# Three of four weight sums from GpSimd to VectorE, and a new order of the VectorE and ScalarE programs in a Strassen-like up projection

## The reference

```python
f_gate, f_val = jnp.split(x @ w_up, 2, axis=-1)          # x: 544 x 1024, w_up: 1024 x 5632
ffn_ext = jnp.concatenate([ffn_hist, f_gate], axis=1)    # two rows of history before the frames
f = gelu(causal_dwconv(ffn_ext, ffn_conv_w, ffn_conv_b)) * f_val      # width 3, 2816 channels
x = layer_norm(DN_ALPHA * x + f @ w_down, ln2_g, ln2_b)
```

## Time and profile before

| | us |
|---|---|
| median of 3 runs | 1791.38 (1789.69 to 1792.2) |
| the profiled execution | 1789.32 |
| its span, first to last instruction | 1787.6 |
| PE busy in the span | 1744.7 (98%) |
| DVE busy | 1372.1 (77%) |
| ACT busy | 856.1 (48%) |
| POOL busy | 350.0 (20%) |

### The profile page before, as it was taken

How to read it: one execution, slowest core, us unless ns; L and a number is a source line. 1 busy time by engine, 2 the same in 40 slices (tenths; PEclk the granted TensorE clock), 3 DMA queues, 4 the chain that set the end, 5 groups by cost and what they waited for, 6 DMA issues and landing times.

```text
span 1787.6 us, 32649 instructions
## 1 busy us (share of the span) xinstructions
PE 1744.7 (98%) x13802; PEld 1702.0 (95%) x13802; DVE 1372.1 (77%) x1869; ACT 856.1 (48%) x1366; POOL 350.0 (20%) x311
## 2 busy tenths in 40 slices
PE   9999999999999999999999999999999999999997
PEld 9998999999998999999999989999999999999997
DVE  5698677755779999876768887786558789998665
ACT  4256533353555555554542564323534655556443
POOL 0025100000135555200000350000001545551000
PEclk9999999999999999999999999999999999999999
DMA  5522122223222222345525221222232222223544
GB/s 173 170 97 72 41 91 74 87 89 97 97 74 88 94 85 83 105 165 179 170 96 170 73 95 36 85 95 71 93 121 72 71 90 79 93 94 111 183 165 137
DMA packets 36514, 186.00 MB, mean 104 GB/s; under 512 B 7376, under 2 KB 11728, under 8 KB 18192
## 3 DMA queue, kind: packets, MB, share of 16 engines
q1 hardware_dynamic: 34672, 176.28, 29.5%
q10 hardware_dynamic: 1696, 7.64, 1.2%
HBM read 176.75 MB, written 7.15 MB: 103 GB/s over the span
## 4 chain that ended last, share of the span: by engine, by line
PE 47%; DVE 10%; issue 4%; POOL 3%; DMA 2%; ACT 2%; ACTq 0%; DVEq 0%; POOLq 0%
PE acc L1995 13%; PE acc L2001 13%; PE acc L2000 13%; DVE cbuf L1763 2%; DMA raw<-wup 2%; DVE slo L1830 2%; DVE fst L1766 2%; POOL sraw L575 1%; PE score L1995 1%; PE score L2001 1%; POOL sraw L578 1%; PE score L2000 1%; DVE wl L1825 1%; DVE cbuf L1769 1%; POOL raw L577 1%
## 5 line engine op out<-in xcount | busy, mean ns | idle before, releaser
L1995 PE MATMUL acc<-xh,wh 128*128 128x272 f32 x1928 | 565.1, 293 | 1.6 <-DVE xl L1163 1.0
L2001 PE MATMUL acc<-xh,wl 128*128 128x272 f32 x1928 | 555.6, 288 | 0.0
L2000 PE MATMUL acc<-xl,wh 128*128 128x272 f32 x1928 | 554.8, 288 | 0.0
L1995 PEld LDWEIGHTS acc<-xh,wh 128*128 128x128 f32 x1928 | 363.1, 188 | 9.7 <-issue 5.0
L1209 DVE TENSOR_TENSOR wl<-raw,wh 128x2048 fp32r<-128x2048 f32 (+2 forms) x118 | 236.1, 2001 | 171.6 <-ACT wh L607 171.0
L2000 PEld LDWEIGHTS acc<-xl,wh 128*128 128x128 f32 x1928 | 363.2, 188 | 0.1
L2001 PEld LDWEIGHTS acc<-xh,wl 128*128 128x128 f32 x1928 | 362.2, 188 | 0.0
L607 ACT ACTIVATE wh<-raw 128x2048 fp32r<-128x2048 f32 (+2 forms) x138 | 236.5, 1714 | 160.8 <-DMA raw<-wdn 113.7
L1995 PE MATMUL acc<-fhh,wh 128*128 128x272 f32 x704 | 204.4, 290 | 2.0 <-DVE wl L1209 2.0
L2000 PE MATMUL acc<-fll,wh 128*128 128x272 f32 x704 | 202.4, 288 | 0.0
L2001 PE MATMUL acc<-fhh,wl 128*128 128x272 f32 x704 | 202.4, 287 | 0.0
(11 more groups left out here) (322 smaller groups left out, 4214.5 us busy)
## 6 DMA issues: line engine op xcount, KB each, us to landing
raw<-win SPq DMA_DIRECT2D x50, 1024.0 KB, 5.0
raw<-wup SPq DMA_DIRECT2D x44, 1024.0 KB, 4.9
raw<-wdn SPq DMA_DIRECT2D x32, 1024.0 KB, 4.8
raw<-wbr SPq DMA_DIRECT2D x24, 512.0 KB, 3.6
raw<-wdn SPq DMA_DIRECT2D x16, 768.0 KB, 4.2
raw<-wout SPq DMA_DIRECT2D x8, 1024.0 KB, 5.0
v_out<-vfm ACTq DMA_DIRECT2D x2, 1088.0 KB, 9.5
k_out<-k ACTq DMA_DIRECT2D x2, 1088.0 KB, 4.9
```

The source lines that it names most:

```text
L1995: first = mm(out, a, xs[0], start=start, stop=False, skip_group_check=onto)
L2000: mm(out, a, xs[1], start=False, stop=False, skip_group_check=onto)
L2001: return mm(out, b, xs[0], start=False, stop=stop, skip_group_check=onto)
```

## The change

GpSimd makes only the first sum s1 of each quad. VectorE makes the other three (third_sum, second_sum, fourth_sum). It has a new wait in first_sum for the chunk, for product 5 of quad q-2 and for GpSimd's sum (s_one). The sums of quad q+2 are issued in quad q, those of 0 and 1 ahead of the loop. ScalarE copies the last gate rows of two tiles at once (last_rows), in place of four VectorE copies; conv_close waits for it (fst_made). The history copy is one instruction for two tiles. ScalarE converts the first half of a chunk before the second, and both engines' lists have a new order.

```diff
-ACT_ORDER, DVE_ORDER = [], []
-for _q in range(QUADS + 1):
-    ACT_ORDER += [("u3", _q - 1)] if _q else []
-    ACT_ORDER += [("m1", _q)] if _q < QUADS else []
-    ACT_ORDER += [("c12", _q - 1)] if _q else []
-    ACT_ORDER += [("u1", _q)] if _q < QUADS else []
-    DVE_ORDER += [("c22", _q - 1)] if _q else []
-    DVE_ORDER += [("c11", _q)] if _q < QUADS else []
+ACT_ORDER, DVE_ORDER = [("m1", 0)], [("c11", 0)]
+for _q in range(QUADS):
+    ACT_ORDER += [("u1", _q), ("u3", _q)]
+    ACT_ORDER += [("m1", _q + 1)] if _q + 1 < QUADS else []
+    ACT_ORDER += [("c12", _q)]
     DVE_ORDER += [("c21", _q - 1)] if _q else []
     DVE_ORDER += [("f", _q - 1)] if _q and _q % 2 == 0 else []
+    DVE_ORDER += [("c22", _q)]
+    DVE_ORDER += [("c11", _q + 1)] if _q + 1 < QUADS else []
+DVE_ORDER += [("c21", QUADS - 1), ("f", QUADS - 1)]
...
                     if q > 1:
                         pool.wait_ge(prod_full, full_at(r, q - 2, 5))
-                    g.tensor_tensor(s1, a21, a22, ALU.add).then_inc(s_made, 1)
-                    pool.wait_ge(s_made, made + 1)
-                    g.tensor_tensor(a21, a11, a21, ALU.subtract).then_inc(s_made, 1)
-                    g.tensor_tensor(s2, s1, a11, ALU.subtract).then_inc(s_made, 1)
-                    pool.wait_ge(s_made, made + 3)
-                    if q > 1:
-                        pool.wait_ge(prod_full, full_at(r, q - 2, 6))
-                    g.tensor_tensor(s4, a12, s2, ALU.subtract).then_inc(s_made, 1)
...
+                    g.tensor_tensor(sraw[q % 2][:, 0, :].rearrange("p (t n) -> p t n", t=4),
+                                    w[:, 0:4, 1, :], w[:, 4:8, 1, :], ALU.add).then_inc(s_one, 1)
...
+                def last_rows(i):
+                    A(fst[:, 2 * i:2 * i + 2, :].rearrange("p m (g r) -> p m g r", r=2),
+                      gex[:, :, GEX - 2 * (DEC + 2):GEX].rearrange("p m (g r) -> p m g r", g=2)[:, :, :, DEC:DEC + 2],
+                      ACT.Copy).then_inc(fst_made, 1)
...
+                first_blocks(0)
                 second_blocks(0)
-                first_blocks(0)
                 two_sums(0)
                 last_sum(0)
+                conv_gelu(0)
                 turned_x_hi(T1, T4N)
-                conv_gelu(0)
                 conv_gelu(1)
...
+                snapshot("m1", 0, 1, "c11")
+                first_blocks(1)
+                second_blocks(1)
+                for q in range(QUADS):
+                    snapshot("u1", q, 3, "c21")
+                    if q % 2:
+                        first_tap(q - 1)
+                    elif q:
                         conv_gelu(1)
                     two_sums(q + 1)
+                    if q == QUADS - 1:
+                        f_his(0, 0)
+                    snapshot("u3", q, 5, "c22")
+                    if q % 2:
+                        conv_gelu(0)
                     last_sum(q + 1)
-                    if q == QUADS - 1:
+                    if q + 1 < QUADS:
+                        snapshot("m1", q + 1, 1, "c11")
+                    else:
                         hi()
...
+                    first_blocks(q + 2)
+                    top_right(q)
+                    second_blocks(q + 2)
+                    if q + 2 == QUADS:
+                        hi()
+                f_his(0, 1)
+                conv_gelu(1)
                 f_his(0, 2)
...
-                        v.tensor_copy(row(fst, t, 0, 2), gex[:, m, SEQ:SEQ + 2]).then_inc(vec, c.up(vec))
-                        v.tensor_copy(row(fst, t, 2, 4), gex[:, m, GEX - 2:GEX]).then_inc(vec, c.up(vec))
+                        if m == 0:
+                            dve.wait_ge(fst_made, c.take(fst_made))
...
+                def third_sum(q):
+                    if q < QUADS:
+                        a11, a12, a21, a22 = blocks_of(q)
+                        v.tensor_tensor(a21, a11, a21, ALU.subtract).then_inc(s_made, 1)
+
+                def second_sum(q):
+                    if q < QUADS:
+                        a11, a12, a21, a22 = blocks_of(q)
+                        v.tensor_tensor(sum_of(q, 1), sum_of(q, 0), a11, ALU.subtract).then_inc(s_made, 1)
...
+                        v.tensor_tensor(sum_of(q, 2), a12, sum_of(q, 1), ALU.subtract).then_inc(s_made, 1)
...
                 turned_x_lo(T2, T3)
+                first_sum(0)
+                third_sum(0)
+                second_sum(0)
+                fourth_sum(0)
+                first_low(0)
+                back_low(0)
                 skip(range(4))
-                conv_close(1, range(2), False)
-                first_low(0)
-                other_lows(0)
+                conv_close(1, (0,), False)
+                two_lows(0)
+                last_low(0)
+                conv_close(1, (1,), False)
                 turned_x_lo(T1, T4N)
+                first_sum(1)
+                third_sum(1)
+                second_sum(1)
+                fourth_sum(1)
+                left(0, 0)
+                first_low(1)
                 f_products(1)
                 history(2)
...
+                for q in range(QUADS):
                     if q:
                         left(q - 1, 1)
...
+                        first_low(q + 1)
+                    back_low(q + 1)
                     if q % 2:
                         conv_close(2 + q // 2, (0,), False)
+                    elif q:
+                        gated_values(q - 1)
+                    bottom_right(q)
+                    if q == QUADS - 1:
+                        f_lows(0, 0)
+                    first_sum(q + 2)
+                    two_lows(q + 1)
+                    third_sum(q + 2)
+                    second_sum(q + 2)
+                    last_low(q + 1)
+                    fourth_sum(q + 2)
+                    if q + 2 == QUADS:
+                        lo()
+                    if q % 2:
+                        conv_close(2 + q // 2, (1,), False)
+                    if q + 1 < QUADS:
+                        left(q + 1, 0)
+                    if q and q % 2 == 0:
+                        history(2 + q // 2)
+                lo()
+                f_lows(0, 1)
+                left(QUADS - 1, 1)
+                gated_values(QUADS - 1)
```

More of the change, by code:

```diff
@@ L347, in trunk @@
         s_made = sem("s_made")
+        s_one = sem("s_one")
         s_hi = sem("s_hi")
+        back_hi = sem("back_hi")
+        fst_made = sem("fst_made")
         s_ready = sem("s_ready")
@@ L562, in _ @@
                     g.tensor_tensor(traw[j][:, :, :], a, b, ALU.subtract).then_inc(t_made, 1)
-                def sums(q):
+                for q in range(QUADS):
                     j = first_chunk(r) + q
[L566 to L571, removed]
+                    s = SLOT[j]
+                    w = raw[s][:, :].rearrange("p (t m n) -> p t m n", t=KT, m=2)
                     pool.wait_ge(raw_full[s], 16 * (SLOT[:j + 1].count(s) - (1 if s < 2 else 0)))
@@ L1000, in first_blocks, with second_blocks @@
                         turn[0] += 1
-                        act.wait_ge(s_made, 4 * (l * QUADS + q) + 2)
+                        act.wait_ge(raw_full[s], c.take(raw_full[s], 16))
+                        act.wait_ge(s_made, 3 * (l * QUADS + q) + 1)
                         A(wh[s][:, 0:CHUNK // 2], raw[s][:, 0:CHUNK // 2], ACT.Copy).then_inc(hi_full[s], c.up(hi_full[s]))
+                def second_blocks(q):
+                    if q < QUADS:
+                        s = SLOT[first_chunk(l) + q]
+                        A(wh[s][:, CHUNK // 2:], raw[s][:, CHUNK // 2:], ACT.Copy).then_inc(back_hi, 1)
                 def two_sums(q):
                     if q < QUADS:
-                        act.wait_ge(s_made, 4 * (l * QUADS + q) + 3)
+                        act.wait_ge(s_made, 3 * (l * QUADS + q) + 2)
                         A(shi[q % 2][:, 0:2, :], sraw[q % 2][:, 0:2, :], ACT.Copy).then_inc(s_hi, 1)
@@ L1032, in first_tap @@
                     act.wait_ge(combined, dve_at(l, "c21", q))
-                    act.wait_ge(gex_full, c.take(gex_full, 2))
+                    act.wait_ge(gex_full, c.take(gex_full))
                     for m in range(2):
@@ L1777, in history @@
                         dve.wait_ge(conv3_full, c.seen(conv3_full))
-                    for m in range(2):
-                        ins = v.tensor_copy(gex[:, m, 2 + SEQ:4 + SEQ], row(fhist, 2 * i + m, 0, 2))
-                        ins.then_inc(gex_full, c.up(gex_full))
+                    v.tensor_copy(gex[:, :, 2 + SEQ:4 + SEQ], fhist[:, 2 * i:2 * i + 2, :]).then_inc(gex_full, c.up(gex_full))
                 def f_products(i, banks=ps):
@@ L1825, in other_lows, with sum_low @@
                         v.tensor_tensor(wl[s][:, n:], raw[s][:, n:], wh[s][:, n:].bitcast(F32), ALU.subtract).then_inc(
                             lo_full[s], c.up(lo_full[s]))
+                def sum_low(q, n, part):
+                    if q < QUADS:
                         i = q % 2
[L1828 to L1831, removed]
```

(39 more changed lines are left out.)

61 lines of the change are left out of this document (19 added, 42 removed).

## The result

The changed kernel takes 1749.88 us (median, 1749.75 to 1750.33), against 1791.2 us for the kernel before: a ratio of 0.977, with a 95% interval of 0.9754 to 0.9787. The forecast was 1754, in a range of 1748 to 1775. The profiled execution spans 1748.4 us, 39.2 less than before. One execution of the kernel before, in the job of the runs e5 to e8, took 2603.9 us at a granted clock of 0.60 and is left out of every comparison.

A forecast was written before the change was run, and what follows sets the result against it. The prediction took VectorE and GpSimd's exclusive SBUF access as the bound. From 41.7 us, 2 x (1.0 + 1.0) and 0.5 were subtracted: 37.2 off 1789.3 gives 1752.1, with 2.1 for the median 1754; range 1748 to 1775.

The forecast's parts named there:

- Ceiling: TensorE's losses inside the quads' stage, before its first product and at the second down chunk, both layers: 41.7 us in total.
- Part 1: Three sums a quad move from GpSimd to VectorE at 0.61 us each; VectorE then wants 20.8 of TensorE's 21.1 us a pair.
- The limit before: In the quads, VectorE and GpSimd exclude each other on SBUF access: 23.1 us wanted a pair against 22.94 measured.
- Part 2: New order inside a quad: nothing late in steady state, smallest margin 0.6 us; late loads cost 0.5 us in all.
- Part 3: Last gate rows: one ScalarE copy per pair of tiles replaces tiny VectorE copies; given no price of its own.
- Part 4: Start of the stage: the 3.0 us wait and the clock loss go; 1.0 us of new wait for u1 in each layer.
- Part 5: End of the stage: u3 wait in quad 17 taken as 1.0 us new; the 1.00 us second down chunk wait goes.
- Sum: Whole kernel: 41.7 less 2 x (1.0 + 1.0) and 0.5 gives 37.2 us gained, 1752.1 profiled, 1754 for the median.
- (a): Rival in the quads: VectorE or ScalarE misses deadlines, a pair loses 1 us, 18 us in all, 1772 us; chance 0.22.
- (b): Rival: strided sums on VectorE cost what they cost on GpSimd, 1822 us; slower than before from 1.0 us a sum; chance 0.07.
- (c): Rival: port sharing makes moving the sums a draw, a pair keeps 22.9 us, 1782 to 1791 us; chance 0.05.
- (d): Rival at the stage's start: the wait stays, three sums standing ahead of the first low; 3.0 + 1.6 us a layer, 1763; chance 0.06.

The follow-up runs named there:

- e5: Kernel before with the three weight sums on VectorE and ScalarE's snapshot u1 moved ahead of the copies of the sums: 1762.31 us, ratio 0.9846.
- e8: Changed kernel with the first weight sum on VectorE as well, so all four are there and GpSimd is idle in the stage: 1748.19 us.
- e10: Changed kernel with the fourth weight sum made twice on VectorE in each quad: 1760.29 us.
- e1: Changed kernel with all four weight sums back on GpSimd, new order kept: 1781.44 us, ratio 0.9962 to the kernel before.
- e9: Changed kernel with one more GpSimd sum of 128x512 per quad into a scratch tile nobody waits for: 1768.67 us, ratio 0.9885.
- e2: Kernel before with only the three weight sums moved to VectorE, in its old order: 1780.29 us, ratio 0.9949.
- e4: Changed kernel with the last gate rows copied by VectorE again, four tiny copies in a pair of quads: 1751.59 us.
- e11: Changed kernel with the fourth weight sum made four times on VectorE in each quad: 1815.38 us, ratio 1.0152.
- e3: Changed kernel with both convolution tiles ahead of the first sums and first low again, as before: 1749.94 us, ratio 0.9779.
- e6: Kernel before with only ScalarE's snapshot u1 moved earlier, the sums still on GpSimd: 1794.89 us, ratio 1.003.

## Why the prediction was right, point by point

- **Ceiling, 41.7 us.** It was made of the stage's length less 126 products. It held: from the first product to the down projection layer 0 takes 192.2 us now, 207.3 before, layer 1 192.3 and 207.0, and the 3.0 us ahead of it and the 1.0 us behind it are gone in both layers.
- **Part 1.** 0.61 us from start to start for a strided sum is what it costs (0.685 by itself, a pitch of 0.60). VectorE's want of 20.8 us a pair was 0.5 too high by e10 (20.3), so the margin is 0.8 and not 0.3. The prediction let GpSimd's two sums stop VectorE for their whole 2.6 us; in e10 they do so for 1.9. The 2.2 us for "the four PSUM sums of a pair" fit the six sums that a pair has, in seven instructions.
- **The limit before.** "I take the exclusion, not any single chain, as the limit" is the step that failed. The exclusion is real and its size is about right (e1 at 22.73 us a pair, e9). The 23.1 us that it was added up to are at least 0.2 too high, since nothing can be held for longer than the period of 22.94. And a chain of 22.4 us lay just under it (e2). The forecast survived, since part 2 took the chain apart by the walk through the deadlines, and since it was made against TensorE's own time and not as a sum of gains of parts. Made part by part, it would have given most of 39 us to part 1, which alone brings 8.5. That the forecast survived is in part luck: the expectation for e2, made from the same reading, ended at 1762 us, and 1780.3 were measured.
- **Part 2.** Nothing is late in steady state, as walked: a pair takes 21.16 us (product 7 at 579.68 and 706.64, six pairs apart, in layer 0). The gated values even run into GpSimd's sum once a pair (1.32 us for the last piece of 0.22), as walked.
- **Part 3.** At no price; measured 1.7 us at most (e4).
- **Part 4.** The walk gave three sums done by 538.9 and the first low by 540.0; the trace has 538.6 and 539.7. The wait for u1 of quad 0 was put at 1.0 and is 0.77, 0.9 with its slow first matmul.
- **Part 5.** Here terms were mis-sized, to the safe side. The wait at product 6 of quad 17 was put at 1.0, and it stayed what it was: TensorE stands still for 0.49 us, before and after. f_his(0,0) ends at 733.98, just in time for u3 at 734.04. Late loads were put at 0.5 us and cost nothing visible.
- **Sum.** Over 126 products 1.9 us are left in layer 0 and 2.1 in layer 1, 4.0 in all, where 4.5 were forecast. The stage and its two ends gave 37.7 us. The other 1.5 us of the 39.2 by which the span fell lie outside every term of the ceiling, 1.0 of them between the two stages of quads, and what brought them stays open. The median lies 4.1 us under the forecast also because 2.1 us were added for the distance of the profiled execution from the median, and the profiled execution of the changed kernel lies 0.45 above its median.
- **Rivals.** (a) didn't come, but is only 0.8 us a pair away: one extra VectorE instruction of 0.7 us in a quad costs 10 us. Its price in the prediction left out the margin of 0.3 that it named: a pair would have lost 0.7 us and not 1. (b) is shown in kind by e11. With a margin of 0.8 the change would, as an estimate, have ended slower from (0.8 + 2.1) / 6 = 0.5 us above 0.61, so 1.1 us a sum, where the prediction had 1.0. (c) fell: moving sums between engines that exclude each other helps because one holds the access 1.29 us for what the other does in 0.61. (d) fell in e3.

## What to carry to other kernels

Add up what an exclusive resource is asked for in a period, by both engines, and set it beside the measured period: here 23.1 against 22.94, equal within the error of such a sum, named a limit that no wait in the profile names. Then walk the in-order lists against the deadlines all the same, since a second limit can lie 0.5 us below the first, and then neither half of a change shows what the whole brings (8.5 and 7.4 of 41 us). Look also at what comes ahead of the chain: the one of e2 starts late because of a copy that GpSimd's sum holds up. The room that an engine has is measured by giving it more to do, not by its idle time.

## What the runs showed of the hardware that I had not expected

- A GpSimd instruction without any reader costs TensorE's stage about 1.0 us a pair for two sums of 1.29 us each (e9). It holds up VectorE, and TensorE waits for that.
- How long TensorE stood still does not say by itself whether its clock falls. In e11 it fell to the lower of its two levels (granted 0.50, 1.2 GHz, matmuls 0.23 us apart in place of 0.125) for 2.5 to 3.2 us behind four of the five waits of 2.8 to 3.0 us and behind three of the five of 2.0 to 2.1 us, and stayed at the upper level behind the others: at 1476.58 a wait of 2.81 us ended and the matmuls went on 0.125 us apart. Behind one of 2.09 us they first took their usual pace for 1.5 us and slowed down then, from 731.60 to 734.78. Behind the waits of 1.3 to 1.8 us, in e11 and in layer 0 of e5, nothing slowed down. The starts of before, e1, e2 and e6, with waits of 3.0 to 3.9 us, all had slow matmuls behind them.
